# Attention value products with stacked high and low parts, and probabilities divided by GpSimd

## The reference

```
scores = einsum('bnqkgd,bnskd->bnkgqs', qb, kb) * (HD ** -0.5)
scores = scores - slopes * dist                # and -inf outside the window
e      = exp(scores - m[..., None])
probs  = e / (e.sum(axis=-1) + exp(sink - m))[..., None]
o      = einsum('bnkgqs,bnskd->bnqkgd', probs, vb)
return o.reshape(b, s, H * HD) @ wo
```

## Time and profile before

| | us |
|---|---|
| median of 3 runs (1076.98 to 1077.5) | 1077.31 |
| the profiled execution | 1077.67 |
| its span in the profile | 1074.3 |
| outside its span | 3.4 |
| TensorE busy | 1057.5 |
| VectorE busy | 782.0 |
| ScalarE busy | 472.7 |
| GpSimd busy | 163.1 |

### The profile page before, as it was taken

How to read it: one execution, slowest core, us unless ns; L and a number is a source line. 1 busy time by engine, 2 the same in 40 slices (tenths; PEclk the granted TensorE clock), 3 DMA queues, 4 the chain that set the end, 5 groups by cost and what they waited for, 6 DMA issues and landing times.

```text
span 1074.3 us, 13753 instructions
## 1 busy us (share of the span) xinstructions
PE 1057.5 (98%) x4936; PEld 876.7 (82%) x4936; DVE 782.0 (73%) x1127; ACT 472.7 (44%) x819; POOL 163.1 (15%) x270
## 2 busy tenths in 40 slices
PE   7899999999999999999999999999999999999998
PEld 5788888877888888888888888888888888888887
DVE  6877777888445599776677668376776878747985
ACT  6566666676323234313232342353333334437451
POOL 8655555443000000000000000000000000001000
PEclk9999999999999999999999999999999999999999
DMA  8111111050332325253344154998988898660102
GB/s 313 45 34 41 40 40 36 25 196 20 122 114 86 109 87 208 118 196 133 148 170 154 81 193 180 382 412 284 290 294 289 285 334 292 248 234 1 40 30 88
DMA packets 67472, 171.79 MB, mean 160 GB/s; under 512 B 5200, under 2 KB 5456, under 8 KB 67280
## 3 DMA queue, kind: packets, MB, share of 16 engines
q1 hardware_dynamic: 67408, 170.95, 44.3%
HBM read 133.18 MB, written 37.75 MB: 159 GB/s over the span
## 4 chain that ended last, share of the span: by engine, by line
PE 89%; DVE 6%; POOL 2%; issue 2%; ACT 1%; ACTq 0%; POOLq 0%; DVEq 0%
PE pair L2520 28%; PE pair L2500 22%; PE pair L2248 10%; PE pair L2385 8%; PE pair L2566 7%; PE pair L2315 3%; PE pair L2458 3%; PE pair L2283 3%; PE pair L2595 2%; PE pair L2294 1%; PE pair L2428 1%; POOL bias L846 1%; PE pair L2267 1%; DVE qT L1561 1%; PE pair L2227 0%
## 5 line engine op out<-in xcount | busy, mean ns | idle before, releaser
L2520 PE MATMUL pair<-uT 128*128 128x512 f32 x1344 | 305.7, 389 | 0.0
L2520 PEld LDWEIGHTS pair<-uT 128*128 128x128 f32 x1344 | 252.0, 188 | 52.3
L1297 ACT ACTIVATE uT<-wo_raw 128x1024 fp32r<-128x1024 f32 x83 | 84.6, 1054 | 112.6 <-PE pair L2520 96.5
L1951 DVE TENSOR_TENSOR uT<-wo_raw,uT 128x1024 fp32r<-128x1024 f32 x83 | 98.5, 1221 | 44.4 <-ACT uT L1297 43.8
L791 POOL TENSOR_SCALAR row_var<-row_ssq 128x1 f32<-128x1 f32 x16 | 4.0, 249 | 706.2 <-ACT hn L1338 623.0
L2385 PE MATMUL pair<-WA,oT 128*128 128x512 f32 x384 | 90.4, 393 | 1.4 <-DVE WA L1708 1.0
L2385 PEld LDWEIGHTS pair<-WA,oT 128*128 128x128 f32 x384 | 71.2, 188 | 16.9 <-issue 2.4
L2500 PE MATMUL pair<-WA,WB 128*128 128x512 f32 x336 | 78.2, 389 | 0.4 <-ACT xr L1272 0.4
L2500 PEld LDWEIGHTS pair<-WA,WB 128*128 128x128 f32 x336 | 63.0, 188 | 13.8 <-DVE WB L1885 0.8
L2566 PE MATMUL pair<-WA 128*128 128x512 f32 x288 | 68.1, 391 | 0.0
L2566 PEld LDWEIGHTS pair<-WA 128*128 128x128 f32 x288 | 53.7, 188 | 11.0
(11 more groups left out here) (241 smaller groups left out, 1876.7 us busy)
## 6 DMA issues: line engine op xcount, KB each, us to landing
wo_raw<-in_m_w SPq DMA_DIRECT2D x71, 512.0 KB, 6.3
wo_raw<-hid_kept SPq DMA_DIRECT2D x41, 512.0 KB, 5.7
hid_kept<-RES SPq DMA_DIRECT2D x32, 512.0 KB, 2.7
emb<-in_m_w SPq DMA_DIRECT2D x17, 512.0 KB, 5.9
RES<-in_m_w SPq DMA_DIRECT2D x8, 1024.0 KB, 6.6
uT_f<-in_m_w SPq DMA_DIRECT2D x6, 1024.0 KB, 6.8
RES<-in_a_wqkv SPq DMA_DIRECT2D x10, 512.0 KB, 8.4
emb<-hid_kept SPq DMA_DIRECT2D x10, 512.0 KB, 5.6
```

The lines of the kernel that those rows point to most:

```text
L1297: nc.scalar.activation(operand(t, which, HI), unit(t, which), ACT.Copy).then_inc(op_hi, 1)
L1951: nc.vector.tensor_tensor(operand(t, which, LO), unit(t, which), operand(t, which, HI).bitcast(F32), ALU.subtract).then_inc(op_ready, 1)
L2520: mm = nc.tensor.matmul(ps[4 * (j % 2) + m][:], operand(t, 0, s)[:, k, m * P:(m + 1) * P], operand(t, 1, r)[:, k, :], start=(g == 0 and k ...
```

## The change

Values are stored as `[key tile, kv head, part, channel]`, so that the high and low part of one head stand side by side as one operand of 128 columns. `weigh_values` multiplies that operand by the high and by the low probabilities: two matmuls a key tile instead of three, four a group instead of six. The result has the high part's product in rows 0 to 63 and the low part's in rows 64 to 127. ScalarE moves both out (four pieces instead of two): the high to `RES`, the low to `ring`. VectorE adds them later, half a block at once (`add_low`), in groups 0 and 2 of the next block. `oT_hi_half` waits for these sums. As `ring` is now used by the attention, the first two loads of the MLP's weights wait for the last sum.

The product with the reciprocal leaves VectorE. GpSimd does it, one instruction of 128x128 a head, and its place in GpSimd's order is: group 0's ahead of the norm of "q8" (in the last block behind it), and group j's ahead of `mask_probs` of group j - 1.

```diff
@@ SP @@
-                sp.dma_start(ring[:, k % 2, :].rearrange("p (k n) -> p k n", k=2), rows_of(w1, k, 0, BANK)).then_inc(ring_in[k % 2], 16)
-                if k == 1:
+                elif k == 0:
                     sp.wait_ge(biased, H * NB)
                     sp.dma_start(xr[:], x[0:P, :]).then_inc(xr_in, 16)
                     load_residual(1)
+                    sp.wait_ge(lows_added, 2 * NB)
+                sp.dma_start(ring[:, k % 2, :].rearrange("p (k n) -> p k n", k=2), rows_of(w1, k, 0, BANK)).then_inc(ring_in[k % 2], 16)
@@ GpSimd @@
+            def scale_probs(n, j):
+                pool.wait_ge(rden_ready, 4 * n + j + 1)
+                for r in range(G):
+                    row = probs[:, j % 2, r, 0:P]
+                    scaled = pool.tensor_scalar(row, row, rden[:, j % 2, r:r + 1], 1.0, ALU.mult, ALU.mult)
+                scaled.then_inc(probs_ready, 1)
...
             def body(n, last=False):
-                head_norm("q8", n)
+                if last:
+                    head_norm("q8", n)
+                scale_probs(n, 0)
+                if not last:
+                    head_norm("q8", n)
                 place_sinks(n, 1)
                 mask_probs(4 * n - 1)
...
                 place_sinks(n, 2)
                 dv_hi_part(n)
+                scale_probs(n, 1)
                 mask_probs(4 * n)
...
                 place_sinks(n, 3)
...
+                scale_probs(n, 2)
                 mask_probs(4 * n + 1)
...
+                scale_probs(n, 3)
                 mask_probs(4 * n + 2)
@@ ScalarE @@
             def attention_out(n, j):
+                if j % 2 == 0:
+                    wait(act, lows_added, 2 * (n - 2) + j // 2 + 1)
                 for odd in range(2):
+                    rows = slice(odd * HD, (odd + 1) * HD)
+                    nc.scalar.activation(flat[rows, bass.ds(n * D + j * 2 * P, 2 * P)],
+                                         pv_bank[0:HD, odd * 2 * P:(odd + 1) * 2 * P], ACT.Copy)
+                    moved = nc.scalar.activation(low_out(n, j * 2 * P, 2 * P)[rows],
+                                                 pv_bank[HD:P, odd * 2 * P:(odd + 1) * 2 * P], ACT.Copy)
@@ VectorE @@
-            def scale_probs(n, j):
-                nc.vector.tensor_tensor(probs[:, i, :, 0:P], probs[:, i, :, 0:P],
-                                        rden[:, i, :].unsqueeze(2).to_broadcast([P, G, P]),
-                                        ALU.mult).then_inc(probs_ready, 1)
...
+            def add_low(n, hf):
+                dve.wait_ge(attended, 4 * n + 2 * hf + 2)
+                o = RES[:, n, hf * BANK:(hf + 1) * BANK]
+                nc.vector.tensor_tensor(o, o, low_out(n, hf * BANK, BANK), ALU.add).then_inc(lows_added, 1)
...
+                    if j in (0, 2) and not first:
+                        add_low(n - 1, j // 2)
@@ TensorE, weigh_values @@
-                    for s, m in PASSES:
+                    for m in (HI, LO):
+                        mm = nc.tensor.matmul(pv_bank[:], vz[:, kt, j, :, :].rearrange("p s d -> p (s d)"), pT[:, m, kt, :],
+                                              start=(done == 0), stop=(done == 3))
```

More of the change, by code:

```diff
@@ L438, in trunk_layer @@
         T_ready = {X: sem(f"{X}_T_ready") for X in PARTS}
+        lows_added = sem("lows_added")
         v_staged = sem("v_staged")
@@ L551, in trunk_layer, with low_out, by_head @@
         turn_bank = ps[6]
+        def low_out(n, at, cols):
+            return ring[:, n % 2, at:at + cols]
+        def by_head(v):
+            return v[:].rearrange("p (v d) -> p v d", d=HD)
         def q_rows(odd, s):
@@ L635, in _ @@
                     load_residual(1)
+                    sp.wait_ge(lows_added, 2 * NB)
+                sp.dma_start(ring[:, k % 2, :].rearrange("p (k n) -> p k n", k=2),
+                             rows_of(w1, k, 0, BANK)).then_inc(ring_in[k % 2], 16)
             def spill_h(b):
@@ L864, in dv_hi_part @@
                     stand(pool, pv_done, 4 * b)
-                copy(vz[:, 0, HI, :], vprev[:]).then_inc(dv_moved, 1)
+                copy(vz[:, 0, :, HI, :], by_head(vprev)).then_inc(dv_moved, 1)
             def keep_v(b):
@@ L920, in _ @@
                     place_sinks(0, 2)
+                    scale_probs(0, 0)
                 if j == 1:
@@ L925, in _ @@
                     place_sinks(0, 3)
+                    scale_probs(0, 1)
                     mask_probs(0)
@@ L930, in _ @@
                     head_norm("k", 1)
+                    scale_probs(0, 2)
                     mask_probs(1)
                 if j == 3:
+                    scale_probs(0, 3)
                     mask_probs(2)
@@ L1016, in v_hi_part @@
                 wait(act, pv_done, 4 * b)
-                nc.scalar.activation(vz[:, 1, HI, :], vnext[:], ACT.Copy).then_inc(v_hi, 1)
+                nc.scalar.activation(vz[:, 1, :, HI, :], by_head(vnext), ACT.Copy).then_inc(v_hi, 1)
             def k_hi_part(b, par):
@@ L1137, in oT_hi_half @@
                     act.wait_ge(x_squared, NB)
-                    act.wait_ge(attended, GROUPS * (b + 1))
+                    act.wait_ge(lows_added, 2 * (b + 1))
                 else:
-                    act.wait_ge(attended, NB * GROUPS)
+                    act.wait_ge(lows_added, 2 * NB)
                 if isinstance(b, int):
@@ L1748, in _ @@
             body(NB - 1, 1, last=True)
+            add_low(NB - 2, 0)
+            add_low(NB - 2, 1)
             pT_lo_part(NB * GROUPS - 1, 1)
@@ L1787, in _ @@
             oT_lo_half(2, 0)
+            add_low(NB - 1, 0)
+            add_low(NB - 1, 1)
             oT_lo_half(2, 1)
@@ L2311, in weigh_values @@
                         pe.wait_ge(v_ready, 2 * n + 2)
-                    for s, m in PASSES:
-                        at = 2 * HD * (j // 2)
-                        mm = nc.tensor.matmul(pv_bank[:], vz[:, kt, s, at:at + 2 * HD], pT[:, m, kt, :],
-                                              start=(done == 0), stop=(done == 5))
+                    for m in (HI, LO):
+                        mm = nc.tensor.matmul(pv_bank[:], vz[:, kt, j, :, :].rearrange("p s d -> p (s d)"), pT[:, m, kt, :],
+                                              start=(done == 0), stop=(done == 3))
                         done += 1
```

13 lines of the change are left out of this document (3 added, 10 removed).

## The result

| | before | after |
|---|---|---|
| median, us (6 runs each, side by side) | 1077.11 (1076.14 to 1077.5) | 1103.26 (1100.86 to 1103.7) |
| ratio, 95% interval | | 1.024 (1.0227 to 1.0253) |
| profiled execution, us | 1077.67 | 1103.38 |
| its span | 1074.3 | 1101.7 |
| outside the span | 3.4 | 1.7 |

The kernel became 26 us slower. The prediction had 1091.5 with a range of 1080 to 1101: the direction was right, the size was little more than half.

What follows compares the result with a forecast made beforehand. It took TensorE (98% busy) as the bound, with the ring of work between engines deciding the gain. Profiled 1077.67 plus 1 (first block), 0.8 (six steady), 12.5 (last) gave 1092.0, or 1091.5 us against the median; range 1080 to 1101.

Steps and rivals of the forecast that it cites:

- TensorE's saving, turned into waits: Steady block: the whole 1.84 us taken from TensorE's work becomes waits ahead of group 2's scores and `turn_q`.
- The division at 1.6 us: GpSimd's four 128x128 products with the reciprocal, per group: 1.6 us, between a low end of 1.31 and a high of 2.24.
- The first block, +1: First block: same order with GpSimd's bias and `scale_x` between, costing +1 us (0 to +2).
- The ring of the steady block, 29.1 us: Steady block: work passed round the engines sets its length, 29.1 us after the change against 29.03 before.
- For six steady blocks I take 0.1 to 0.15 each with some contention: +0.8 us: Six steady blocks: each 0.1 to 0.15 us longer with some contention, +0.8 us in all.
- The last block, the order of masks and divisions: Last block: masks queued behind the next group's products close a ring for every group, about 8.3 us a group.
- The sign: Last block: TensorE idle 3 us or more a group for GpSimd's mask before the value matmuls in groups 0 to 2.
- Last block: +12.5 us: Last block: delayed turns cost 13.1 us, less 0.5 saved on TensorE, giving +12.5 us (10 to 15).
- The handover at 0: Hand-over to the MLP: its first weights load after the last sum, costed at 0, up to 3 us without cover.
- A: Rival: steady blocks do gain, their ring being 1.9 us shorter than counted; 1080 us, chance 0.12.
- B: Rival: masks come in time in the last block too, so the kernel is faster; 1063.6 us, chance 0.08.
- C: Rival: port lock, products at 2.24 us in eleven places (7 us) and 0.6 in six blocks; 1102 us, chance 0.12.

Runs made afterwards that it cites:

- e3: Kernel before with only the stacked values, four pieces and late sums, the division staying on VectorE and GpSimd's old order: 1078.62 us, ratio 1.0016.
- e1: Changed kernel with GpSimd's two-input product on x_cols moved to the start of the block: 1105.02 us, ratio 1.0264.
- e7: Changed kernel with the norm of "q8" ahead of group 0's division in every block: 1094.47 us, ratio 1.0162.
- e8: Changed kernel with GpSimd's product on x_cols moved behind the copy of the values' difference: 1100.6 us, ratio 1.0218.
- e2: Changed kernel with each mask ahead of the next group's division in the last block: 1093.42 us, ratio 1.0154.
- e5: Changed kernel with 124 unused transposes filling TensorE's idle time in the last block: 1098.25 us, ratio 1.0205.
- e11: Changed kernel with VectorE's weight units 6 and 7 waiting for GpSimd's last division: 1098.85 us, ratio 1.02.

## Why the prediction was right in direction and wrong in size

- **TensorE's saving, turned into waits: right.** A wait of 1.61 us ahead of group 2's scores where 1.4 was said. The prediction's own two times, 14.95 and 13.8, make it 1.15. Its 20.3 for `turn_q` should be 19.9, as three groups' values lie before it and not two. Neither touches the 29.1, which came through VectorE. The wait of 0.5 ahead of `turn_q` didn't appear. e3 shows the eaten saving too: 1.84 us a block less work by the forecast, 0.25 us less time.
- **The division at 1.6 us: right**, a little high (1.43).
- **The first block, +1: right,** with 0.8.
- **The ring of the steady block, 29.1 us: right where nothing blocks.** 29.05 in block 6, and 29.02 in the later block of e1 that escapes. The late sum's 0.44 us beside a mask lies in it too; the division, 0.17 shorter than said, takes back a part.
- **"For six steady blocks I take 0.1 to 0.15 each with some contention: +0.8 us": this term failed.** It measured 6.7. The new order put the 4-column `nmax` of group 1 under GpSimd's 1.90 us product, 1.27 us in each of five blocks; by it `turn_q` stood at 23.01 and not at 21.75. I had looked for contention where large operations meet and left out small ones: a blocked operation costs what the other has left to run, not a share of its own length. e1, e7 and e8 show it. The sentence ahead of the prediction that the engines meet only at semaphores is too strong for this reason: VectorE and GpSimd hold each other up with no semaphore between them.
- **The last block, the order of masks and divisions: right in mechanism.** It was the step on which most hung; the ring came out at 8.19 us where 8.4 was said, and e2 took 9.8 us back by the order alone. The sign, a wait for the mask of 3 us or more in groups 0 to 2, came in two of the three: 4.65, 2.45 and 6.47.
- **"Last block: +12.5 us": this term failed too.** It measured 19.4. Of the 6.9 between, 1.9 lie between the turns of groups 0 and 1, 2.5 between those of groups 2 and 3, and 2.4 behind the last turn. The clock is missing, 5.0 us by e5: I costed TensorE's stretches at full-clock durations although I had forecast the idle time in front of them. And the last division meets the weight units: I added 0.5 where the products grew by 2.5; e11 took 2.8 back in the profiled execution, 2.0 of them between the last two turns. (The parts overlap, as each run was taken against the changed kernel.)
- **The handover at 0: right.** Behind the last values the span grew by 0.6 us.
- **The rivals.** A and B did not come. C (1102) named blocking and came out within 1.3 us of the result, but its terms were others: the products were not slow in eleven places, and the late sum's 0.44 us was the smaller part.

The rule in the Trainium skill, SBUF - State Buffer (SBUF: two separate sides), that the first of the two to start holds the shared ports for the whole instruction, against an operation of VectorE with two inputs in SBUF, would have priced this had I applied it to `nmax`. The changed kernel agrees: the product starts 0.49 us ahead, and `nmax` ends within 0.02 us of it. In e1 `nmax` is blocked (1.97 us instead of 0.17) although its own record starts 0.06 ahead, so the records there don't tell which was first. And taken for every GpSimd instruction the rule prices too high here: in six blocks the late sum starts under GpSimd's power over 4 columns (176.86 and 176.29 above) and takes 0.68.

## What to carry to other kernels

Before moving work to GpSimd, list who stands behind it in GpSimd's queue and which operations with two SBUF inputs VectorE runs at that time, the tiny ones on the chain first: price each at up to the rest of the GpSimd instruction that it may meet. Where you forecast that TensorE will idle, price what follows at the lower clock as well. And the hand-written order alone took the changed kernel from 1103.3 to 1077.0, so try the order before judging the engine. It stayed 2.3 us above the version with the division on VectorE: the move to GpSimd gained nothing here.

## What was not expected of the hardware

- A VectorE operation on 128x4 took 0.16 us, or 1.43 and 1.97 us beside a two-input product of GpSimd; in e1 leads of 0.06 and 0.07 us by the records went with the one and the other. An operation with one input, the sum of squares over 128x512, took 0.68 beside the same product in e1, as it does without it.
- After the same wait of 2.0 us TensorE's granted clock stayed at 1.00 in one block of e1 and fell in two others (0.71 and 0.72 over 5 us).
- The blocking works both ways: four GpSimd products of 1.42 us together took 3.94 beside two weight units, and when the units came later a mask took 1.62 instead of 0.64.
- Filling TensorE's idle time with 124 unused transposes made the kernel 5.0 us faster.
